# Delta rule block: scalings of the turned k on ACT, first solve level in other banks, chunk-wise waits, one triangle finished in PSUM

## What is computed

```python
decay = exp(where(tri, G[i] - G[j], -inf))
m = where(strict, (k * beta) @ k.T * decay, 0)
sol = triangular_solve(m + eye, [v * beta, k * beta * exp(G)])
w_val, k_cd = sol[..., :dv], sol[..., dv:]
attn = (q @ k.T) * decay
# per chunk, in order:
v_new = w_val - k_cd @ S
o = (q * exp(G)) @ S + attn @ v_new
S = S * exp(G_last) + (k * exp(G_last - G)).T @ v_new
```

## Time and profile before

| | us |
|---|---|
| median of 3 runs | 3461.9 |
| lowest and highest run | 3459.14, 3462.3 |
| the profiled execution | 3458.91 |
| its span in the profile | 3457.1 |
| PE busy in the span | 3104.2 (90%) |
| DVE busy | 1563.1 (45%) |
| POOL busy | 1019.2 (29%) |
| ACT busy | 702.8 (20%) |
| mean granted clock of PE, share of 2.4 GHz | 0.948 |

### The profile page before, as it was taken

How to read it: one execution, slowest core, us unless ns; L and a number is a source line. 1 busy time by engine, 2 the same in 40 slices (tenths; PEclk the granted TensorE clock), 3 DMA queues, 4 the chain that set the end, 5 groups by cost and what they waited for, 6 DMA issues and landing times. The chain is left out here.

```text
span 3457.1 us, 53969 instructions
## 1 busy us (share of the span) xinstructions
PE 3104.2 (90%) x22788; PEld 2938.1 (85%) x22788; DVE 1563.1 (45%) x2621; ACT 702.8 (20%) x1257; POOL 1019.2 (29%) x666
## 2 busy tenths in 40 slices
PE   5997798969999999995999948988769999999996
PEld 4996565959999999983999947777759999999995
DVE  2127366444344343443666645554254344443444
ACT  1002276121010010103121223443021001010002
POOL 1220100323332223313233235665314223322220
PEclk7998899979999999997999979999789999999998
DMA  4100100211111111102233223331302111111101
GB/s 150 44 18 17 31 1 26 76 37 49 45 54 43 39 42 47 52 1 89 70 100 95 76 74 84 76 81 43 109 19 58 41 43 43 56 43 38 43 25 53
DMA packets 251733, 184.13 MB, mean 53 GB/s; under 512 B 47695, under 2 KB 236477, under 8 KB 251269
## 3 DMA queue, kind: packets, MB, share of 16 engines
q1 hardware_dynamic: 251525, 181.09, 17.8%
HBM read 147.19 MB, written 33.84 MB: 52 GB/s over the span
## 5 line engine op out<-in xcount | busy, mean ns | idle before, releaser
L144 PE MATMUL ps<-xhi,whi 128*128 128x364 f32 (+1 forms) x3528 | 1165.6, 330 | 139.2 <-POOL wlo L137 68.1
L145 PE MATMUL ps<-xlo,whi 128*128 128x364 f32 (+1 forms) x3528 | 1164.7, 330 | 0.0
L150 PE MATMUL ps<-xhi,wlo 128*128 128x364 f32 (+1 forms) x3528 | 1163.9, 330 | 0.0
L144 PEld LDWEIGHTS ps<-xhi,whi 128*128 128x128 f32 (+1 forms) x3528 | 662.6, 188 | 147.1 <-POOL wlo L137 68.9
L145 PEld LDWEIGHTS ps<-xlo,whi 128*128 128x128 f32 (+1 forms) x3528 | 663.0, 188 | 4.0 <-issue 0.9
L150 PEld LDWEIGHTS ps<-xhi,wlo 128*128 128x128 f32 (+1 forms) x3528 | 662.4, 188 | 3.6 <-issue 0.9
L1504 DVE TENSOR_TENSOR z<-ps,z 128x364 f32<-128x364 f32 x528 | 283.3, 537 | 640.0 <-PE ps L150 640.0
L1425 POOL TENSOR_SCALAR whi<-wraw 128x1024 fp32r<-128x1024 f32 x132 | 144.6, 1095 | 1041.3 <-PE ps L150 1036.7
L144 PE MATMUL ps<-ff_hhi,whi 128*128 128x364 f32 x1056 | 347.6, 329 | 0.6 <-DVE z L1504 0.6
L150 PE MATMUL ps<-ff_hhi,wlo 128*128 128x364 f32 x1056 | 347.1, 329 | 0.0
L145 PE MATMUL ps<-ff_hlo,whi 128*128 128x364 f32 x1056 | 346.4, 328 | 0.0
(11 more groups left out here) (359 smaller groups left out, 3737.3 us busy)
## 6 DMA issues: line engine op xcount, KB each, us to landing
wraw<-in_w_ff_in SPq DMA_DIRECT2D x88, 512.0 KB, 3.9
wraw<-in_w_ff_out SPq DMA_DIRECT2D x44, 512.0 KB, 3.6
qkvz<-oin_out SPq DMA_DIRECT2D x32, 546.0 KB, 2.9
wraw<-in_w_in_o SPq DMA_DIRECT2D x32, 512.0 KB, 4.3
residual<-z SPq DMA_DIRECT2D x2, 4368.0 KB, 11.8
z<-residual SPq DMA_DIRECT2D x6, 1456.0 KB, 8.9
wraw<-in_w_in_e SPq DMA_DIRECT2D x17, 512.0 KB, 3.9
dn_gb<-gates SPq DMA_DIRECT2D x34, 128.0 KB, 3.6
```

Source lines behind the costliest of these rows:

```text
L144: one = pe.matmul(out, whi, xhi, start=start, stop=False)
L145: two = pe.matmul(out, whi, xlo, start=False, stop=False)
L150: return pe.matmul(out, wlo, xhi, start=False, stop=stop)
```

## The change

ACT does `vb` before the decays eg and egl. kbg is no longer computed by DVE: ACT does it as eight scalings of 128 columns, four per chunk, each four behind DVE's ktl of that chunk; ktl is done in two halves. ACT's square of B's output moves from ahead of the levels to behind the X copies of level 1. On DVE, the product with `low` is no longer written to T but back into PSUM bank 6, behind TT and MT, and T is that plus EYE; the add of EYE to TT moves behind new values 1. The X product of level 1 is written to banks 0 and 1 (the old values' banks), so it waits for new values 1 instead of the second state sum; the wait for the state sum moves to level 2, and the one for kbg to between X and Y of level 1. The final kcd product waits for TT chunk by chunk.

```diff
+    X_BANK = [None, 0] + [4] * (LEVELS - 2)
...
                 if A:
 
-                    pe.wait_ge(s("MT"), A.th(1, 1))
-                    pe.wait_ge(s("Ta"), A.th(2, 2))
+                    pe.wait_ge(s("T0"), A.th(1, 1))
                     pe.wait_ge(s("AT"), A.th(1, 1))
                     turn(A, 6, kk, "kturned")
...
                     if B:
-                        pe.wait_ge(s("S"), B.th(3, 2))
-                    else:
-                        pe.wait_ge(s("vb"), A.th(1, 1))
-                    pe.wait_ge(s("kscaled"), A.th(1, 1))
-
+                        pe.wait_ge(s("vn"), B.th(B.nb, 2))
                     for l in range(1, LEVELS):
                         pe.wait_ge(s("ML"), A.th(l, LEVELS - 1))
+                        if l == 2:
+
+                            if B:
+                                pe.wait_ge(s("S"), B.th(3, 2))
+                            else:
+                                pe.wait_ge(s("vb"), A.th(1, 1))
                         for b in range(A.nb):
...
-                                ins = pe.matmul(bank1(4 + b)[half, j, :], ML[half, l - 1, j, :], T[half, j, :],
+                                ins = pe.matmul(bank1(X_BANK[l] + b)[half, j, :], ML[half, l - 1, j, :], T[half, j, :],
                                                 start=True, stop=True)
                             ins.then_inc(s("X"), 1)
+                        if l == 1:
+
+                            pe.wait_ge(s("kscaled"), A.th(A.nb, 2))
+                            pe.wait_ge(s("kbg"), A.th(1, 1))
...
-                    pe.wait_ge(s("TT"), A.th(A.group(LEVELS - 1, A.nb - 1), 2 * LEVELS))
...
-                    settle(pe, s("settled_pe"))
-
                     for b in range(A.nb):
+                        pe.wait_ge(s("TT"), A.th(A.group(LEVELS - 1, b), 2 * LEVELS))
+                        settle(pe, s("settled_pe"))
...
+            def squares_o(B):
+                act.wait_ge(s("o"), B.th(len(B.blocks()), 2))
+                act.activation(sq[:, :, 0:B.n], bank2(2, B.n), ACT.Square).then_inc(s("osq"), 1)
...
-                    act.wait_ge(s("in_eg"), A.th(32, 32) if n == P else 32 * NPAIR + 16)
-                    nb = len(A.blocks())
-                    act.activation(eg[:, 0:nb], eg[:, 0:nb], ACT.Exp).then_inc(s("eg"), 1)
-                    act.wait_ge(s("eg"), A.th(1, 1))
-                    act.copy(egl[:, A.odd, 0:nb, :], eg[:, 0:nb, :, L - 1:L].squeeze(3)).then_inc(s("egl"), 1)
-
                     act.wait_ge(s("vturned"), A.th(1, 1))
...
                     ins.then_inc(s("vb"), 1)
-                if B:
-                    act.wait_ge(s("o"), B.th(len(B.blocks()), 2))
-                    act.activation(sq[:, :, 0:B.n], bank2(2, B.n), ACT.Square).then_inc(s("osq"), 1)
+
+                    act.wait_ge(s("in_eg"), A.th(32, 32) if n == P else 32 * NPAIR + 16)
+                    nb = len(A.blocks())
+                    act.activation(eg[:, 0:nb], eg[:, 0:nb], ACT.Exp).then_inc(s("eg"), 1)
+                    act.wait_ge(s("eg"), A.th(1, 1))
+                    act.copy(egl[:, A.odd, 0:nb, :], eg[:, 0:nb, :, L - 1:L].squeeze(3)).then_inc(s("egl"), 1)
+
+                    act.wait_ge(s("kturned"), A.th(1, 1))
+                    if B:
+
+                        act.wait_ge(s("vn"), B.th(B.nb, 2))
+                    for b in range(A.nb):
+                        act.wait_ge(s("kscaled"), A.th(b + 1, 2))
+                        settle(act, s("settled_act"))
+                        for j in range(GR * b, GR * (b + 1)):
+                            ins = act.mul(kbg[:, j, :], bank2(6)[:, j, :],
+                                          m.bcol[:, bass.ds(A.index, 1), j:j + 1].squeeze(1))
+                    ins.then_inc(s("kbg"), 1)
+                if B and not A:
+                    squares_o(B)
                 if A:
                     for l in range(1, LEVELS):
                         for b in range(A.nb):
...
-                            act.copy(X[:, hs, :], bank1(4 + b)[:, hs, :]).then_inc(s("Xs"), 1)
+                            act.copy(X[:, hs, :], bank1(X_BANK[l] + b)[:, hs, :]).then_inc(s("Xs"), 1)
+                        if B and l == 1:
+                            squares_o(B)
...
-                    dve.tensor_tensor(T[:, 0:J], bank1(6)[:, 0:J], low[:, 0:J], ALU.mult).then_inc(s("Ta"), 1)
                     dve.wait_ge(s("upl"), A.th(1, 1))
-                    dve.tensor_tensor(TT[:, 0:J], bank1(6)[:, 0:J], upl[:, 0:J], ALU.mult).then_inc(s("Ta"), 1)
+                    dve.tensor_tensor(TT[:, 0:J], bank1(6)[:, 0:J], upl[:, 0:J], ALU.mult).then_inc(s("TTa"), 1)
                     dve.tensor_tensor(MT[:, 0:J], bank1(6)[:, 0:J], ups[:, 0:J], ALU.mult).then_inc(s("MT"), 1)
+                    dve.wait_ge(s("TTa"), A.th(1, 1))
+                    dve.wait_ge(s("MT"), A.th(1, 1))
+                    dve.tensor_tensor(bank1(6)[:, 0:J], bank1(6)[:, 0:J], low[:, 0:J], ALU.mult).then_inc(s("Ta"), 1)
                 if B:
                     state_add(B, 0)
                 if A:
-                    dve.wait_ge(s("Ta"), A.th(2, 2))
-                    dve.tensor_tensor(TT[:, 0:J], TT[:, 0:J], masked(m.EYE, J), ALU.add).then_inc(s("TT0"), 1)
-                    dve.tensor_tensor(T[:, 0:J], T[:, 0:J], masked(m.EYE, J), ALU.add).then_inc(s("T0"), 1)
+                    dve.wait_ge(s("Ta"), A.th(1, 1))
+                    dve.tensor_tensor(T[:, 0:J], bank1(6)[:, 0:J], masked(m.EYE, J), ALU.add).then_inc(s("T0"), 1)
...
                 if B and B.n == P:
                     new_values(B, 1)
                 if A:
+                    dve.tensor_tensor(TT[:, 0:J], TT[:, 0:J], masked(m.EYE, J), ALU.add).then_inc(s("TT0"), 1)
 
                     dve.wait_ge(s("kturned"), A.th(1, 1))
-                    if B:
-
-                        dve.wait_ge(s("vn"), B.th(B.nb, 2))
-                    dve.tensor_tensor(kbg[:, 0:J], bank2(6)[:, 0:J],
-                                      m.bcol[:, bass.ds(A.index, 1), 0:J].squeeze(1).unsqueeze(2).to_broadcast([P, J, P]),
-                                      ALU.mult)
-                    dve.tensor_tensor(ktl[A.odd][:, 0:J], bank2(6)[:, 0:J],
-                                      upi[:, 0:J, L - 1:L].to_broadcast([P, J, P]), ALU.mult).then_inc(s("kscaled"), 1)
+                    for b in range(A.nb):
+                        dve.tensor_tensor(ktl[A.odd][:, HALVES[b]], bank2(6)[:, HALVES[b]],
+                                          upi[:, HALVES[b], L - 1:L].to_broadcast([P, GR, P]), ALU.mult)\
+                           .then_inc(s("kscaled"), 1)
```

More of the change, by code:

```diff
@@ L2443, in run @@
                         if l == 1 and C:
-                            dve.wait_ge(s("kscaled"), A.th(1, 1))
+                            dve.wait_ge(s("kscaled"), A.th(A.nb, 2))
                             dve.wait_ge(s("AT"), A.th(1, 1))
```

## The result

The changed kernel takes **3433.3 us** (median of 4 runs, 3431.3 to 3434.5); the kernel before, run beside it, takes 3460.5 (4 runs, 3458.2 to 3462.3). The ratio is 0.9921, 95% interval [0.9904, 0.9938]: 27 us faster, where 10.75 was forecast. The profiled execution took 3431.3, its span is 3429.1 (3457.1 before).

A forecast was written before the change was run, and what follows sets the result against it. PE was taken to bound the kernel, POOL next. First stage 2.0, six stages at 1.2, ninth-stage entry 1.05 and ninth stage 0.5 sum to 10.75 us saved, giving 3451.2 us; range 3440 to 3459.

The forecast's parts named there:

- the bound of 1.22: DVE's product into PSUM: upper time bound, 0.60 us taken; at 1.22 the gain would sum to 6.5 us.
- Where it is given back: Levels 1 to 3: clips held by POOL delay level 2's subtracts, leaving 0.8 of Y1's 1.84 us gain.
- The alternation: DVE and POOL: two-SBUF-input adds and tensor_scalar wait for a running POOL operation, then go ahead of its next one.
- Rival A: Levels 1 to 3: POOL does not hold the clips; POOL's chain binds at 1.75 us a stage, gain 15 us; chance 0.18.
- Rival B: DVE can't get between queued POOL products; level 2 starts at 28.2, total 8 us slower, 3470; chance 0.08.
- POOL as second bound: End of stage: POOL's chain to `olo` allows 1.2 us a stage, about level with PE's 1.25; 1.2 taken.
- Rival C: Whole kernel: no measurable change, lower-clock stretches or PSUM writes at their bound leave under 6.9 us; chance 0.20.
- Loss 1: State step 0 starts 0.65 us late, waiting on `vb` behind ACT's exp(eg) and its copy.
- Loss 2: The turn of k starts 0.46 us late on AT, because T+EYE took 2.38 us.
- rival D: Edit of T buys nothing by itself, PE being only 0.46 us late at the turn; no separate chance given.
- Loss 3: First X product waits 1.74 us for the second state sum, behind kbg and ktl on DVE.
- Loss 4: The kcd product waits 0.61 us for the second chunk's last TT subtract; chunk-wise waiting saves 0.45.

The follow-up runs named there:

- e9: Changed kernel with DVE doing state sum 0 ahead of the product written back to PSUM: 3431.0 us, ratio 0.9913 to the kernel before.
- e2: Changed kernel with POOL forming the masks' products (ML) of levels 4 and 5 right behind those of 2 and 3: 3442.2 us, ratio 0.9946.
- e10: Changed kernel with PE's squares_sum, and what follows it on ACT and DVE, one level later: 3453.6 us, ratio 0.9979.
- e11: Changed kernel with squares_sum one level later (e10) and ML 4 and 5 formed early (e2): 3435.3 us, ratio 0.9923.
- e5: Kernel before the change, with only ACT's `vb` moved ahead of the decays: 3462.1 us, ratio 1.0002.
- e6: Changed kernel with the product with `low` written to T in SBUF and EYE added there, DVE order kept: 3436.4 us, ratio 0.9930.
- e3: Changed kernel with level 1's X products back in banks 4 and 5, waiting for the second state sum: 3438.3 us, ratio 0.9934.
- e4: Changed kernel with kbg back on DVE as one product ahead of ktl, ACT's eight scalings gone: 3432.0 us, ratio 0.9915.
- e7: Changed kernel with kcd waiting once for TT of both chunks again: 3441.4 us, ratio 0.9940.
- e1: The changed kernel run again, unaltered (the repetition), against the kernel before: 3437.3 us, ratio 0.9932.
- e8: Changed kernel with the edits of e2 and e9, and kbg shared, first half on ACT, second on DVE: 3434.7 us, ratio 0.9921.
- e13: Changed kernel with state sum 0 first (e9) and kbg on DVE (e4): 3428.3 us, ratio 0.9904.
- e12: Changed kernel with state sum 0 first (e9), ML 4 and 5 early (e2) and kbg on DVE (e4): 3432.5 us, ratio 0.9917.
- e14: Changed kernel with state sum 0 first (e9) and ML 4 and 5 early (e2), kbg left on ACT: 3434.9 us, ratio 0.9922.

## Why the prediction was wrong

The sign, the mechanisms and the early part of the stage were right; the size was not: 10.75 us forecast, 24 to 27 measured.

1. **The front of the stage.** State step 0 6.82 (forecast 6.75), state sum 0 8.94 (8.9), X1 16.06 (16.35), Y1 17.92 (17.97). Right, within 0.3 us. The cost of the wait ahead of the PSUM product was put at 0.12; start to start it is 0.79 (2214.20 to 2214.99), where 0.60 is an unwaited step: 0.19. In e9, where the product's follower T+EYE waits for it, 0.73. The Trainium skill ("VectorE: DVE Perf Modes", The DRAIN you can't avoid) has a semaphore behind each of eight copies cost nothing extra; here both places show 0.13 to 0.19 us. One reading of this part missed, without effect: TT+EYE was to end at 12.7, and ended at 13.91 (1.80 us), it seems because POOL's next product, and not the add, came in behind Sg; nothing waited for it. The PSUM write itself is free, so the bound of 1.22 falls.

2. **The step that failed is "Where it is given back".** It had level 2's subtracts at 25.4, X3 at 25.95 and 0.8 of 1.84 us left. Measured: 24.51, 25.02, and 1.87 of 1.89 left (1.6 to 2.0 over the seven stages). Two terms made this. ACT's square of B's output started at 17.66, not 18.3, since the scalings ended at 17.30, not 17.5, and the two X copies behind them took 0.70 together, so POOL's sum started at 18.85, not 19.4; and of the subtraction and the clips, which ended at 21.76, 23.18 and 24.59, the last was a further 0.3 us sooner against POOL. With that, the whole collision just fits under `squares_sum`. I had named this cover and then let the late subtract outlast it by 0.9 us; in truth it outlasted it by 0.0 to 0.1 us (X3 at 25.0 to 25.2 in five stages, 24.9 in four of e2's). That it fits so closely is luck of these lengths and not a rule. e10 and e11 show that the cover decides: 13.8 us at X3, 18.3 in all.

The alternation itself is right: the clips took what was foretold to a tenth or so, and the subtraction, for which 1.6 us stood, took 1.05 because POOL's sum ended sooner, and ended 0.55 behind it. Rival A (clips not held) falls: 1.39 and 1.49 us beside POOL in the changed kernel, 0.43 and 0.42 in e2 and e11, where POOL is through. The Trainium skill ("SBUF — State Buffer", Who interferes with whom) lets two-input SBUF work and tensor_scalar exclude POOL; by that rule the traces agree. What mattered was not whether a collision comes but whether the engine that sets the time, PE, has to wait for it. Rival B falls too: level 2 starts at 24.51, not at 28.2.

3. **POOL as second bound.** The forecast held the period at 39.0, with `olo` ending at 40.96. POOL's q product started at 24.27 instead of 25.4, `olo` ended at 40.03, and Ln is led by PE. The clean period is 37.8 to 38.2: 2.0 to 2.4 a stage, not 1.2. Over stages 1 to 7, 17.55 us against 8.25. Of these 14.3 are seven times 2.04 (40.24 less 38.2), and 3.3 are what before's other stages had over its clean one and the changed kernel's have less of: the stretch at the lower clock (1.4 us) and stops inside matmul runs. Neither was in the sum. Rival C had counted on chance stretches against the gain; the one there was fell away.

4. **The parts.** Loss 1 (`vb`) is worth nothing alone (e5). Loss 2 comes from the place of TT+EYE and not from PSUM (e6): rival D, that the edit of T buys nothing by itself, holds. Loss 3 has two cures, kbg off DVE or X1 in other banks; the change makes both, and either does most of it (e3, e4). Loss 4 is worth 0.6 (e7).

5. **The ends.** The first stage gave 4.3 us for 2.0: X1 came 3.7 us sooner from the opening (forecast 2.46), but Y1 only 2.1 (forecast 2.0), and one stretch of 3.4 us at the lower clock near 2095, which costs half of that, is not in the changed kernel's trace. That share rests on where the low stretches fall: the first stage took 36.7 in the repetition. Behind the ninth opening 3.7 us went for 0.5: the changed kernel and e1, e4 and e6 have 1069.2 to 1070.2 there, but e8, e10 and e11, with the same work, 1072.8 to 1073.9, so most of it is not tied to the change. The stretch at the lower clock there is 34.1 us in the changed kernel, 37.6 before and 41.0 in those three, though also in e13, which has 1069.6. What lies ahead of the block is chance, as far as seen (2.4 us, the same work; all kernels open at 2052.5 to 2058.5).

The 28.0 us between the spans thus add up from the 10.75 of the forecast, 6.0 more in the seven clean periods (point 2 and the kcd wait), 3.3 of stages with stalls, 2.3 more in the first stage, 3.2 more behind the ninth opening and 2.4 ahead of the block. The failed step explains about a third of the 17 us that were missed; the rest is in terms that the sum put too low or at nothing.

6. **The range.** Its low end came from the case of no collision at all, 18.5 us (3443), and the spread of the median. Every case for a gain over 14 us was bound to "the clips are not held". That the clips are held and covered was in no case, though the cover stood in the text; and the ends were not given a spread of their own.

## What to carry to other kernels

When work on a second engine becomes late, work out first what the engine that sets the time does at that moment: a collision of 2 us under a 2 us matmul group costs 0.1 us a stage at most, and 14 us over a block once that group is moved, 18 with the stretches at the lower clock that come with it (e10). Of several edits made together, the ones that empty the engine's path (a freed bank, an add moved behind a result that others wait for) carry the gain, and shifts of load between two helper engines may cost: here undoing one (e4) and swapping two neighbours (e9) made the version with the lowest time. Give each cover its own case in the range, in both directions.

## What the runs showed of the hardware

- PE can stop for 0.3 to 3 us inside a run of matmuls without any wait, and it does so at fixed places of its program, one per 256 instructions: 76 of 77 such stretches lie there, and 75 end 1.2 to 1.6 us after a 16,384-byte packet of the instruction queue has landed. Idle time put to "issue" adds up to 2 us in the block before and to 9 us in e8, e12 and e14, which is as much as these should have won. Why the packets come late there stays open.
- An idle stretch of PE of 1.9 us in every stage (e10) came with short stretches at the lower of the clock's two levels (1.2 for 2.4 GHz) in four of seven stages; e11, in which ML 4 and 5 are formed early and PE has no such idle time, has none. e8's trace shows them too, at 2198 and 2239, just behind its stops of 2.97 and 2.1 us.
- The first stage's low-clock share differs from kernel to kernel between 3.4 and 17.1 us. It was the same in the two kernels of before's order (13.7 us, and 3.4 more near 2095), but e6 and e7 have the 13.7 too, and the changed kernel and its repetition differ (10.2 and 6.8): how much of it belongs to the order stays open.
- A DVE product of 128 x 512 written to PSUM takes 0.70 us, to SBUF 0.68.
